# First attention layer: values stationary on two column halves, probabilities divided by GpSimd, TensorE's step as scores, first turn, mix, second turn

## What is computed

```python
def ab_layer(u, w_in, ...):
    ...
    o_a = dsa_mixer(aq, ackv, akr, aqi, aki, awi, w_uk, w_uv)   # 8 heads of 64, keys picked by an indexer
    o_b = fox_mixer(bq, bk, bv, bf + b_forget)                  # 8 heads of 64, with a decay per head
    o = jnp.concatenate([o_a.reshape(b, s, -1), o_b.reshape(b, s, -1)], axis=-1)
    return o @ w_out
```

## Time and profile before

| | us |
|---|---|
| three timed runs | 907.1, 907.37, 908.17 |
| median | 907.37 |
| span of the profiled execution, first to last instruction | 906.0 |
| own time of the profiled execution | not given; the timed runs lie 1.1 to 2.2 above the span |
| TensorE busy | 888.7 (98% of the span) |
| VectorE busy | 645.3 (71%) |
| ScalarE busy | 509.7 (56%) |
| GpSimd busy | 124.6 (14%) |
| the stage of the mixers, from the scores of step 2 to the end of the first half of the output projection | 92.02 to 130.13 |

### The profile page before, as it was taken

The page is one execution under the profiler, slowest core; times in us unless marked ns, Lnnn a source line. Parts: engine busy times, 40 slices in busy tenths (PEclk is TensorE's granted clock), DMA queues, the critical chain, the costliest instruction groups (busy, mean ns, idle before and its releaser), DMA issues. The chain is left out here.

```text
span 906.0 us, 14857 instructions
## 1 busy us (share of the span) xinstructions
PE 888.7 (98%) x4796; PEld 743.3 (82%) x4796; DVE 645.3 (71%) x1305; ACT 509.7 (56%) x1017; POOL 124.6 (14%) x168
## 2 busy tenths in 40 slices
PE   8999999999999999999999999999999999999998
PEld 7878787888888888888878888888887778878876
DVE  4768756766666679787467666666876878777785
ACT  6653836445444456686354444444656666666573
POOL 1310300000000000355010000000530401400401
PEclk9999999999999999999999999999999999999999
DMA  9643143656555557101437665555464445454431
GB/s 336 226 150 114 31 157 116 209 191 197 193 188 197 193 186 232 48 25 48 140 116 223 195 189 192 198 185 191 142 221 144 140 140 184 149 179 141 163 116 47
DMA packets 41609, 145.75 MB, mean 161 GB/s; under 512 B 4688, under 2 KB 6224, under 8 KB 41552
## 3 DMA queue, kind: packets, MB, share of 16 engines
q1 hardware_dynamic: 41264, 144.93, 48.2%
q10 hardware_dynamic: 288, 0.07, 0.0%
HBM read 143.93 MB, written 1.05 MB: 160 GB/s over the span
## 5 line engine op out<-in xcount | busy, mean ns | idle before, releaser
L463 DVE TENSOR_TENSOR wl<-raw,wh 128x1024 fp32r<-128x1024 f32 (+2 forms) x270 | 329.3, 1223 | 89.7 <-ACT wh L458 87.0
L458 ACT ACTIVATE wh<-raw 128x1024 fp32r<-128x1024 f32 (+2 forms) x270 | 281.7, 1046 | 66.0 <-PE acc L355 43.3
L353 PE MATMUL acc<-wh,xhl 128*128 128x512 f32 (+1 forms) x472 | 190.8, 404 | 1.3 <-DVE wl L463 0.9
L355 PE MATMUL acc<-wh,xhl 128*128 128x512 f32 (+1 forms) x472 | 184.6, 391 | 0.0
L354 PE MATMUL acc<-wl,xhl 128*128 128x512 f32 (+1 forms) x472 | 184.0, 390 | 0.0
L353 PEld LDWEIGHTS acc<-wh,xhl 128*128 128x128 f32 x472 | 88.7, 188 | 25.8 <-issue 8.0
L355 PEld LDWEIGHTS acc<-wh,xhl 128*128 128x128 f32 x472 | 88.6, 188 | 19.1
L354 PEld LDWEIGHTS acc<-wl,xhl 128*128 128x128 f32 x472 | 88.9, 188 | 16.3
L353 PE MATMUL acc<-wh,hh 128*128 128x512 f32 x256 | 100.2, 392 | 0.0
L354 PE MATMUL acc<-wl,hh 128*128 128x512 f32 x256 | 100.0, 391 | 0.0
L355 PE MATMUL acc<-wh,hl 128*128 128x512 f32 x256 | 99.7, 390 | 0.0
(11 more groups left out here) (302 smaller groups left out, 1350.5 us busy)
## 6 DMA issues: line engine op xcount, KB each, us to landing
raw<-stream SPq DMA_DIRECT2D x266, 512.0 KB, 3.4
raw<-stream SPq DMA_DIRECT2D x4, 352.0 KB, 6.5
h<-x SPq DMA_DIRECT2D x4, 256.0 KB, 4.0
out<-h SPq DMA_DIRECT2D x3, 256.0 KB, 2.1
row<-rows SPq DMA_DIRECT2D x1, 700.0 KB, 9.4
probs<-sel SPq DMA_DIRECT2D x1, 512.0 KB, 8.3
cst<-consts SPq DMA_DIRECT2D x1, 507.0 KB, 7.6
out<-h SPq DMA_DIRECT2D x2, 128.0 KB, 2.0
```

Of the source, the lines that this page charges most:

```text
L353: nc.tensor.matmul(out_, ah, bh, start=start, stop=False, skip_group_check=True)
L355: return nc.tensor.matmul(out_, al, bh, start=False, stop=stop_, skip_group_check=True)
L458: nc.scalar.activation(used(u, wh[:, u % SPLIT, :]), used(u, raw[:, u % RAW, :]), ACT.Copy).then_inc(w_hi, 1)
L463: nc.vector.tensor_tensor(used(u, wl[:, u % SPLIT, :]), used(u, raw[:, u % RAW, :]), used(u, wh[:, u % SPLIT, :]).bitcast(F32), ALU.subtra ...
```

## The change

The mix of the AB layer is turned around. The values of one head, 128 x 64, are stationary now, on columns 0 to 63 for head 0 and 64 to 127 for head 1, and the turned probabilities move, 256 and 128 columns (`o_mix`). The result has features on partitions, two heads in one tile of 128 x 256, in `misc` or `acc[3]` in turn; this is the form that the output projection wants, so ScalarE copies it to `xh[:, st]` (`o_to_high`) and VectorE subtracts to `xl[:, st]` (`o_to_low`), and the turns of `o_tok` are gone. Since queries lie along the free axis, the division can't be done behind the mix; VectorE takes the reciprocals of the sums (`reciprocals`) and GpSimd multiplies the probabilities by them before they are turned, in four instructions a step. The second turn has a bank of its own, `acc[2]`. TensorE's order in an iteration is scores, first turn, mix, second turn. The last iteration and the last mix stand behind the first two output units, which wait for the steps two by two. The blocks of turns behind it are counted anew (`B_M0` and so on), the waits of the C layer on `s_mixed`, `s_scaled` and `s_coef` too.

```diff
-                if block_b is not None:
-                    pe.wait_ge(hi_out, 4 * block_b + uu + 1)
+                if steps or block_b is not None:
+                    if steps:
+                        pe.wait_ge(o_high, 2 * uu + 2)
+                    else:
+                        pe.wait_ge(hi_out, 4 * block_b + uu + 1)
...
-                            pe.wait_ge(lo_out, 4 * block_b + uu + 1)
+                            if steps:
+                                pe.wait_ge(o_low, 2 * uu + 2)
+                            else:
+                                pe.wait_ge(lo_out, 4 * block_b + uu + 1)
...
+
+        def turned_bank(st, a):
+
+            return acc[2] if st < STEPS_AB and a == 1 else ptp
+
+        def ab_out(st):
+
+            return (misc, acc[3])[st % 2][:, 0:SEQ]
+
+        def mixed(eng, steps):
+
+            if steps > STEPS_AB:
+                eng.wait_ge(s_mixed, steps - STEPS_AB)
+            else:
+                eng.wait_ge(o_mixed, 2 * steps)
 
...
             def turn_p(st, a):
 
-                pe.wait_ge(s_exped, 2 * st + a + 1)
-                pe.wait_ge(s_copied, 2 * st + a)
+                if st < STEPS_AB:
+                    pe.wait_ge(p_normed, 2 * st + a + 1)
+                    pe.wait_ge(s_copied, 2 * st)
+                else:
+                    pe.wait_ge(s_exped, 2 * st + a + 1)
+                    pe.wait_ge(s_copied, 2 * st + a)
                 pb = probs[:, st % DEEP, :]
                 for k, c0 in enumerate((a * P, 2 * P + a * SEQ, 3 * P + a * SEQ)):
-                    last = nc.tensor.transpose(ptp[:, k * P:(k + 1) * P], pb[:, c0:c0 + P], ident)
+                    last = nc.tensor.transpose(turned_bank(st, a)[:, k * P:(k + 1) * P], pb[:, c0:c0 + P], ident)
                 last.then_inc(s_turned, 1)
 
+            def o_mix(st):
+
+                pe.wait_ge(s_copied, 2 * st + 2)
+                if st >= 2:
+                    pe.wait_ge(o_low, st - 1)
+                v = ab_values(st)
+                for s in range(2):
+                    for a in range(2):
+                        last = mm(ab_out(st)[a * HD:(a + 1) * HD, s * P:SEQ], v(a)(s),
+                                  c_pt(st, a)[:, 2 * s * P:SEQ + s * P], start=s == 0, stop=s == 1,
+                                  skip_group_check=True)
+                        if s == 1:
+                            last.then_inc(o_mixed, 1)
+
             def mix(st, v):
 
...
             def ab_iter(it):
 
+                if it == DEEP:
+                    pe.wait_ge(ev_act, left(G_ABO))
+                    pe.wait_ge(ev_dve, left(G_ABO))
+                if it < STEPS_AB:
+                    ab_scores(it)
                 if 0 <= it - DEEP < STEPS_AB:
                     turn_p(it - DEEP, 0)
-                if it < STEPS_AB:
-                    ab_scores(it)
-                if it >= STEPS_AB:
-                    mix(it - DEEP - 1, ab_values(it - DEEP - 1))
+                if it > DEEP:
+                    o_mix(it - DEEP - 1)
                 if 0 <= it - DEEP < STEPS_AB:
                     turn_p(it - DEEP, 1)
-                if DEEP < it < STEPS_AB:
-                    if it == DEEP + 1:
-                        pe.wait_ge(ev_act, left(G_ABO))
-                        pe.wait_ge(ev_dve, left(G_ABO))
-                    mix(it - DEEP - 1, ab_values(it - DEEP - 1))
 
             def between(u):
 
@@ -1091,22 +1134,23 @@
...
-            for it in range(2, STEPS_AB + DEEP):
+            for it in range(2, STEPS_AB + DEEP - 1):
                 ab_iter(it)
-                if it in (STEPS_AB, STEPS_AB + 1):
-                    pe_turn_block(pe, 1, o_tok, (it - STEPS_AB,))
+
+            def scores_read(uu):
+
+                if uu == 0:
+                    pe.wait_ge(s_peaked, 2 * STEPS_AB)
 
             def ab_output(uu):
 
                 if uu == 0:
-                    mix(STEPS_AB - 1, ab_values(STEPS_AB - 1))
-                    pe_turn_block(pe, 1, o_tok, (2,))
+                    ab_iter(STEPS_AB + DEEP - 1)
                 if uu == 1:
-                    pe.wait_ge(s_scaled, STEPS_AB)
-                    pe_turn_block(pe, 1, o_tok, (3,))
-            output_and_turn(G_ABO, U_ABO, 1, 0, ab_output)
-
-            mlp(0, U_M0, 2, 0, 3, H_AB)
+                    o_mix(STEPS_AB - 1)
+            output_and_turn(G_ABO, U_ABO, None, 0, ab_output, B_M0, scores_read)
...
+            def o_to_high(st):
+
+                act.wait_ge(o_mixed, 2 * st + 2)
+                s_.activation(xh[:, st, :], ab_out(st), ACT.Copy).then_inc(o_high, 1)
...
                         act_turn_block(act, b, gain, (uu - 5,), KD)
                 act_turn_block(act, b, gain, (2, 3), KD)
@@ -1622,24 +1670,29 @@
             for it in range(1, STEPS_AB + DEEP):
                 if 0 <= it - DEEP < STEPS_AB:
                     p_first(it - DEEP)
+                if it - DEEP >= 2:
+                    o_to_high(it - DEEP - 2)
                 if it - 1 < STEPS_AB:
                     exponentials(it - 1)
                 if 0 <= it - (STEPS_AB - 3) < LEAD:
                     split(U_ABO + it - (STEPS_AB - 3))
...
-            for it in range(STEPS_AB):
-                coefficients(it).then_inc(s_coef, 1)
+            for st_ in range(STEPS_AB):
+                pool.wait_ge(p_recip, st_ + 1)
+                for a in range(2):
+                    for t, _, n in TK:
+                        c0 = t * 2 * P + a * n
+                        last = g.tensor_scalar(probs[:, st_ % DEEP, c0:c0 + n], probs[:, st_ % DEEP, c0:c0 + n],
+                                               c_stat(rs, st_)[:, a, t:t + 1], None, ALU.mult)
+                    last.then_inc(p_normed, 1)
             mlp_rstd(N_M0, 2)
...
                 dve.wait_ge(s_turned, 2 * st + 2)
                 if st >= 2:
-                    dve.wait_ge(s_mixed, st - 1)
-                v_.tensor_copy(c_pt(st, 1), ptp[:, 0:KEYS]).then_inc(s_copied, 1)
+                    mixed(dve, st - 1)
+                v_.tensor_copy(c_pt(st, 1), turned_bank(st, 1)[:, 0:KEYS]).then_inc(s_copied, 1)
...
-
-                scaled(st, o_tok[:, :, 2 * HD * st:2 * HD * (st + 1)].rearrange("p t (a d) -> p a t d", a=2), rs)
+            def reciprocals(st):
+
+                dve.wait_ge(s_exped, 2 * st + 2)
+                v_.reciprocal(c_stat(rs, st), c_stat(su, st)).then_inc(p_recip, 1)
+
+            def o_to_low(st):
+
+                dve.wait_ge(o_high, st + 1)
+                v_.tensor_tensor(xl[:, st, :], ab_out(st), xh[:, st, :].bitcast(F32), ALU.subtract).then_inc(o_low, 1)
 
             for it in range(STEPS_AB + DEEP):
+                if 0 <= it - 2 < STEPS_AB:
+                    reciprocals(it - 2)
                 if 0 <= it - DEEP < STEPS_AB:
                     p_second(it - DEEP)
-                if it < STEPS_AB - 1:
+                if it < STEPS_AB:
                     ab_peaks(it)
-                if it > DEEP:
-                    ab_scaled(it - DEEP - 1)
-                if it == STEPS_AB - 1:
-                    ab_peaks(it)
+                if it - DEEP >= 2:
+                    o_to_low(it - DEEP - 2)
                 if 0 <= it - (STEPS_AB - 2) < LEAD:
                     split(U_ABO + it - (STEPS_AB - 2))
-                if it in (STEPS_AB, STEPS_AB + 1):
-                    dve_turn_block(dve, 1, ccs=(it - STEPS_AB,))
                 if it == 0:
```

More of the change, by code:

```diff
@@ L355, in mm3, with pe_group @@
             return nc.tensor.matmul(out_, al, bh, start=False, stop=stop_, skip_group_check=True)
-        def pe_group(pe, g, u0, n, w, k0=0, block_b=None, free=None, after=None, ready=None, close=True, late=False):
+        def pe_group(pe, g, u0, n, w, k0=0, block_b=None, free=None, after=None, ready=None, close=True, late=False, steps=False):
             for uu in range(n):
                 u = u0 + uu
-                pe.wait_ge(w_lo if block_b is None else w_hi, u + 1)
+                pe.wait_ge(w_hi if steps or block_b is not None else w_lo, u + 1)
                 if ready is not None:
@@ L788, in keep_clock, with output_and_turn @@
                     mm(bank[:, :], zero[:, 0:P], zero[:, :], start=True, stop=True, skip_group_check=True)
-            def output_and_turn(g, u0, b, h0, behind):
-                pe_group(pe, g, u0, 4, GW, block_b=b, after=behind)
+            def output_and_turn(g, u0, b, h0, behind, next_b, ready=None):
+                pe_group(pe, g, u0, 4, GW, block_b=b, after=behind, ready=ready, steps=b is None)
                 def turn(uu):
@@ L1120, in turn_compress @@
                     last.then_inc(pe_prep, 1)
-            pe_group(pe, G_C, U_C, 4, CQ, block_b=3, after=lambda uu: turn_rest(3, H_AB, uu), late=True)
+            pe_group(pe, G_C, U_C, 4, CQ, block_b=B_A1, after=lambda uu: turn_rest(B_A1, H_AB, uu), late=True)
             pe_group(pe, G_C + 1, U_CQ, 4, GW, after=turn_compress)
@@ L2040, in scaled, with output_and_turn @@
```

(9 more changed lines are left out.)

82 lines of the change are left out of this document (48 added, 34 removed).

## The result

The changed kernel takes 911.78 us (median of 12 runs, 910.48 to 913.85), the kernel before on the same chips 907.83. The ratio is 1.0041, interval [1.0031, 1.005]. The prediction was 905.8 us with a range of 904.2 to 910.4, and held "slower by over 0.2%" for the least likely of its three cases.

The account below looks back on a forecast made before the run. TensorE, busy 888.7 of 906.0 us, was taken as the bound. The stage's end, 115.0 + 11.23 + 2.38 = 128.6 against 130.13, gave 1.5 us less: 905.8 off the median 907.37, range 904.2 to 910.4.

Parts of the forecast that it names:

- Added: New work on GpSimd, VectorE and ScalarE; GpSimd's multiplications taken at 0.90 us a head, bounds 0.60 and 1.64.
- the sign of being right: GpSimd's multiplications of 128 and 256 columns would show near 0.32 and 0.55 us.
- Rival D: GpSimd's division is the bound, at over 1.3 us a head: 908 to 910 us, near 909; chance 0.12.
- The walk: TensorE traced step by step through the changed stage, which would end at 128.6 against 130.13, 1.5 us less.
- its slopes: Each 0.1 us more a head on GpSimd costs about 0.3 us up to 1.2 a head, 1 us beyond.
- the ring: From the third mix, TensorE waits for VectorE's copy, peaks and subtraction before reusing the mix's bank: 3.50 us a step.
- Opening: Stage start: turns wait for GpSimd's first divisions, starting at 95.5 and 96.4; TensorE waits 0.5 twice, 0.2 us gained.
- Mix: TensorE's mix, four products with the two heads pairing on column halves: 0.80 us taken, bounds 0.75 and 1.40.
- rival C: Column halves do not pair, so each mix from step 4 on costs 1.40 us: 910.4 us; chance 0.20.
- Steps at 2.52: Two TensorE steps after the opening, each scores, two turns and mix, at 2.52 us against 2.95.
- Last step and tail: Loop's last step: first output unit at 115.0 against 116.90; last turns and mixes behind it 2.38 us, stage end 128.6.
- Rival B: The wait on VectorE's subtraction costs less, GpSimd fast, pairing complete: 904.2 to 905.0 us, near 904.7; chance 0.13.

Follow-up runs that it names:

- e2: Changed kernel plus products of zeros, read by nobody, filling TensorE's waits in the opening and last steps to hold the clock: 909.65 us, ratio 1.0023.
- e3: Changed kernel, but VectorE divides head 0 and GpSimd head 1 alone: 908.85 us, ratio 1.0012; 906.7 us in its runs at full clock.
- e9: Changed kernel, but GpSimd divides only each head's 256 columns, leaving the other 128 undivided: 906.62 us; 906.53 in its runs at full clock.
- e10: Changed kernel, but both heads' mix products write to the first column half, the second head's in other columns of the bank: 913.47 us.
- e1: Changed kernel, but GpSimd does not divide, two tiny fills a step replacing its four multiplications: 905.42 us, ratio 0.9978.
- e11: Changed kernel with only the splits of the first output weights moved later on ScalarE and VectorE: 911.18 us; 908.7 in its runs at full clock.
- e8: Changed kernel with VectorE dividing head 0, VectorE's subtraction ahead of the peaks, and later splits of the first output weights: 903.37 us, ratio 0.9949.

## Why the prediction was wrong

**The step that failed** is the price of a head on GpSimd, in "Added": 0.90 us "since the factor is read from memory", against 1.49 measured (its two instructions took 0.60 and 0.92 where 0.32 and 0.55 were the sign of being right). The bounds, 0.60 and 1.64, held it; the choice between them did not. I leaned on a copy and a conversion, and on the multiplication having one input of that size. It costs nearly what the two-input product of the earlier trace rows costs (0.64 for 128 columns; here 0.60, and 0.92 for 256). Rival D named this, at a chance of 0.12, and gave 908 to 910; at full clock it is 909.65. The walk would have come out nearly right with the right price: by its slopes 1.49 a head ends at 132.4, and e2's stage of 40.14 us, begun at 92.02, ends at 132.2. (The "132.7" for 1.64 a head does not follow from these slopes, which give 133.9.) Its reason for the steep slope was wrong, though: GpSimd's two heads, 2.98 us, do not close the ring of 3.53; they are paid for in the opening, in the steps before the ring and in the last steps. The Trainium skill (GPSIMD Engine Reference, 4.1 Engine selection) says to keep elementwise work off GpSimd, but counts one-input operations there as roughly at line rate. The traces agree with the advice and not with the exception: 643 and 923 ns in the mean, against 286 and 461 for the same instruction on VectorE in e3.

**The step that was missing** is the clock. It stood at 1.00 in the earlier trace rows, and no rival asked what new waits do to it. It is 2.1 us by e2, and moves the time from the upper part of the range to outside of it. It is TensorE's idling that brought it down: with the waits filled it stayed up in all ten runs. Of the 6.0 us between the forecast and the time, 3.1 are GpSimd's price (e2 against e9), 2.1 the clock, and 0.7 are left; the starting value, 907.37 from three runs where the kernel before otherwise shows 907.5 to 907.9, is part of them, and the rest stays open. The Trainium skill (TensorE: Matmul & The Clock Gate, HAM oscillation — how this bites in real kernels) says that waits between bursts let the clock fall back and that the work after them then runs at the lower level; this trace agrees, with a turn at 0.90 in place of 0.55 behind the waits of 0.84 and 0.93 and two more behind those of 1.37, though these waits are shorter than those of the page's example.

Point by point, the rest. *Opening*: turns at 95.5 and 96.4 forecast; 95.37 and 96.85 measured with the stage 0.58 earlier, so late by 0.4 and 1.0, GpSimd's price of one head and of two. *Mix*: 0.80 taken, 0.81 measured, though the two heads' passes start up to 0.04 us apart where 0.02 was the sign; rival C falls, and e10 shows what it would have been (1.41; 913.5 us where 910.4 was worked out, since GpSimd's price comes on top). *Steps at 2.52*: the scores after the next second turn start at 104.08, 2.61 after those at 101.47: each of the two turns takes 0.47 (102.33 to 102.80) where 0.43 was taken. *Ring from the third mix*: 3.50 taken, 3.53 measured, released by `xhl` as said. *Last step and tail*: right by e9, at the price taken. *Rival B* falls: the ring was no shorter. That the chances gave slower 0.27 in all was too little for a change that adds waits on TensorE, where each one can have a second price that no row of the kernel before shows.

## What to carry to other kernels

When work moves to a slow engine, take its price from the slowest row of the same width there, not from a copy, and find the price at which that engine begins to pace the stage: below it errors cost little, beyond it several times as much (here 1.5 and 5.5 us for each us a head). When a change puts waits of about a microsecond on TensorE, count their second price, work at half clock behind them, as a rival of its own. And where an order is cramped, look at the queues of the engines that release it: here moving six splits was worth 2.4 to 3.2 us, about as much as moving half the division (2.9). A slow engine's instruction can also take longer when another engine's long one is running as it starts, so look at the longest of a form and not at the mean alone.

## What the hardware showed that was not expected

Two products on the two column halves overlap whether they are issued in turn or one head after the other (0.81 us either way, 1.41 on one half), so neighbours in the queue need not be on different halves. GpSimd's multiplication of 128 columns takes 598 to 612 ns in the changed kernel, but for the one beside the split, and 737 to 749 in all eight cases of e3, each of which starts while VectorE runs its own multiplication; that the two are cause and effect was not tried. The clock's fall is not the same in each run of one kernel: e1, e3, e9 and e11 have runs at 1.00 and at 0.994 of the same program, 2.4 to 3 us apart in the medians, while the changed kernel fell in every run and e8 in none. The kernel before has such runs too, one at 0.994 and 911.5 to 912.2 us in each of its sets of 17 to 28. What decides it in a single run stays open.
